# Linear attention in pieces between the units of softmax attention, and a merge added in PSUM

## The chip, the cores and the metric

One core of a Trainium2 chip runs the whole model in one launch. The metric is the device time of the kernel in microseconds; three runs of the kernel before took 2956.83, 2958.68 and 2958.93 us, so their median is 2958.68.

## The reference

Two models run one after the other on 256 tokens of width 1024. The first has 16 meta tokens ahead (272 rows) and two layers, each of feed-forward, mixer, feed-forward; the second has a convolution, sparse attention and two mixtures of 64 experts, and is not touched here. The change is in the first model's mixer and in the norm ahead of it.

```python
def mixer(z, ...):
    h = z @ w_in                       # z = rmsnorm of the residual stream
    (q_a, k_a, v_a, r_a, lr_f, lr_b, q_b, k_b, v_b, g_a, g_b) = jnp.split(h, SPLIT_POINTS, axis=-1)
    a = gla_branch(q_a, k_a, v_a, r_a, lr_f, lr_b, ...)      # linear attention, 4 heads, both directions
    b = attention_branch(q_b, k_b, v_b, ...)                 # softmax attention, 8 heads, 2 key heads
    y = (jax.nn.sigmoid(g_a + b_merge[0]) * (a @ w_pa)
         + jax.nn.sigmoid(g_b + b_merge[1]) * (b @ w_pb))
    return y @ w_out
```

In the linear branch each head (keys of 64, values of 128) is worked out in chunks of 64 tokens: masked scores of queries against keys inside a chunk, and a state S that is decayed and added to from chunk to chunk, once forwards and once backwards. The sum of the two directions is divided by the root of its mean square over the head's 128 values, multiplied by a gain and by silu(r).

## The kernel before, in words

All is float32. Activations lie with features on partitions and the 272 tokens in the free dimension, a tensor of width 1024 as eight tiles of 128 x 272. The five engines have one instruction stream each, written out by hand in one order; semaphores join them. `products` on TensorE runs groups of matmuls into one PSUM bank and then signals it full; `claim` waits until the reader of a bank has freed it. A float32 matmul shows in the trace as two rows.

The feed-forward parts, the merge's projections and the output projection split each number into a rounded high part and a low rest and add three fast products (`split_sum`, its matmuls are line 537). Their weights come in column chunks: SyncE loads a label of the plan into one of three ring buffers once the label three before it is used up, ScalarE rounds a chunk to its high part (`high_part`, line 1073), GpSimd subtracts that from the weights (`low_parts`, line 1826), TensorE multiplies. There are high buffers for three chunks, so chunk c + 3 starts when chunk c is used up. For the feed-forward part the last stage is the down projection: four column pairs c, each in two halves h, two tiles dt. VectorE adds each finished tile to the residual H (line 1450), ScalarE squares it (line 1077).

The mixer of a layer then goes, on TensorE:

- `rms_norm`: `column_means` multiplies the eight squared tiles by a matrix of 1/1024 (line 569) into bank 7; ScalarE takes the root (line 1097), VectorE the reciprocal and the normed tiles (lines 1400 and 1402).
- The projections of w_in, 98 us, and beside them the decays of the linear branch on ScalarE and VectorE. In layer 0 ScalarE also issues eight stores of a bias table (line 1166).
- Softmax attention in 24 units, a head by three tiles of its rows (128, 128, 16). Step n of the loop issues the scores of unit n + 1, the transposes of unit n - 1 (`turn_rows`, line 511), the value products of unit n - 2 (`values`, line 708), and in two of three steps one whole gate tile (`gate_tile`, 8 matmuls of 272 columns). VectorE takes the row maximum (line 1513), ScalarE the exponential (line 1222), VectorE scales it (line 1520) and copies the transposes. The value products of a pair of heads gather in bank 4 or 5. ScalarE turns each gate tile into a sigmoid (line 1171).
- Linear attention, all behind the last unit: transposed decayed keys in three banks, chunk scores of either direction in two (masked on VectorE, line 1535), the meta tokens' scores, the chunk states (chained on VectorE, line 1555), then the outputs of the four heads (line 791) in four banks, 18 small matmuls each, one set over rows 0 to 63 and one over rows 64 to 127.
- The norm of the heads: ScalarE squares each head (line 1237), four products with a matrix of 1/128, four square roots, and per head on VectorE a reciprocal (line 1560), the scaling (line 1562), a rounded and an unrounded product with silu(r) (lines 1564, 1565) and their difference (line 1566).
- The merge: column pair kk of a @ w_pa and of b @ w_pb in turn, four banks. Per tile VectorE multiplies both by their gates (lines 1571 and 1573), adds them (line 1574), rounds the sum (line 1575) and subtracts (line 1576). Then the output projection, eight tiles in banks 4 to 7, added to H (line 1581).

## Time and profile before

| | before |
|---|---|
| runs, us | 2956.83, 2958.68, 2958.93 |
| profiled execution, us | 2959.34 |
| its span, us | 2957.5 |
| mean granted TensorE clock | 0.944 |
| busy, share of the span | TensorE 90%, weight loads 68%, VectorE 35%, ScalarE 31%, GpSimd 31% |
| chain that ended last | TensorE 76%, DMA 11%, VectorE 9%, ScalarE 2% |

The span runs from the first instruction to the last. Matmul and weight load are two rows of one engine and overlap. The granted clock is a share of 2.4 GHz and has two levels, 1.00 and 0.50 (1.2 GHz); a number between them is a mean over a stretch. The chain that ended last is followed backwards from the last instruction, at each step to what released it.

### The profile page before, as it was taken

What the parts mean: (1) busy time and instruction counts of PE and PEld (TensorE: products, weight loads), DVE (VectorE), ACT (ScalarE), POOL (GpSimd) and SP (SyncE); (2) the same over time, 40 slices, a digit from 0 to 9 for tenths busy, and PEclk for the clock granted to TensorE, in tenths of its full rate; (3) what the DMA queues carried; (4) which work ended last, traced back from release to release, by engine and by line L of the source; (5) the groups of instructions that cost most, each with busy time, mean ns of one, the idle gap of its engine ahead of it and who ended that gap; (6) DMA issues with size and microseconds to landing.
All of it is one profiled execution on the core that took longest, in us unless ns stands there. A gap on an engine that the chain in (4) does not pass through costs nothing.

```text
span 2957.5 us, 44948 instructions
## 1 busy us (share of the span) xinstructions
PE 2649.1 (90%) x18090; PEld 2025.6 (68%) x18090; DVE 1049.0 (35%) x2379; ACT 907.9 (31%) x1477; POOL 902.6 (31%) x373
## 2 busy tenths in 40 slices
PE   8999897899999999789989699999878678999996
PEld 8996566899999756679989644444457574444443
DVE  3402424643441152364317333232324623323233
ACT  4431461343443136234433121211113521121112
POOL 6860001588788000147868100000014240000000
PEclk9999996999999999689999799999988988999999
DMA  7553410454554322035545499999952156999995
GB/s 244 160 166 111 128 63 23 132 180 148 182 176 155 127 86 86 29 99 158 164 143 168 171 394 421 421 421 421 421 193 101 43 204 244 421 421 421 421 421 218
DMA packets 271164, 643.95 MB, mean 218 GB/s; under 512 B 16816, under 2 KB 191024, under 8 KB 221616
## 3 DMA queue, kind: packets, MB, share of 16 engines
q1 hardware_dynamic: 267952, 635.66, 57.2%
q10 hardware_dynamic: 2176, 3.15, 0.4%
q0 software_dynamic: 896, 3.15, 0.3%
q8 instruction: 104, 1.70, 0.2%
q14 instruction: 36, 0.29, 0.0%
HBM read 637.72 MB, written 4.19 MB: 217 GB/s over the span
## 4 chain that ended last, share of the span: by engine, by line
PE 76%; DMA 11%; DVE 9%; ACT 2%; issue 1%; SPq 0%; ACTq 0%; POOL 0%; DVEq 0%
PE bank L537 35%; PE bank L501 15%; DMA wring<-in_exp_w 11%; PE bank L997 6%; PE bank L982 5%; PE bank L958 3%; PE bank L1006 3%; PE bank L971 3%; PE bank L791 2%; PE bank L569 2%; PE bank L708 1%; PE bank L511 1%; DVE ARENA L1776 1%; DVE XN_rounded L1425 1%; DVE ARENA_rounded L1576 1%
## 5 line engine op out<-in xcount | busy, mean ns | idle before, releaser
L1826 POOL TENSOR_TENSOR wring_rounded<-wring,wring_rounded 128x1024 fp32r<-128x1024 f32 (+1 forms) x336 | 874.1, 2615 | 438.5 <-ACT wring_rounded L1073 437.8
L537 PE MATMUL bank<-SQ_rounded,wring_rounded 128*128 128x272 f32 (+1 forms) x3456 | 653.7, 289 | 28.4 <-POOL wring_rounded L1826 17.8
L537 PEld LDWEIGHTS bank<-SQ_rounded,wring_rounded 128*128 128x128 f32 x3456 | 545.2, 190 | 30.7 <-POOL wring_rounded L1826 13.8
L1073 ACT ACTIVATE wring_rounded<-wring 128x1024 fp32r<-128x1024 f32 (+1 forms) x336 | 374.5, 1117 | 425.8 <-PE bank L537 420.3
L537 PE MATMUL bank<-XN_rounded,wring_rounded 128*128 128x272 f32 (+1 forms) x1728 | 497.5, 288 | 0.0
L537 PE MATMUL bank<-ARENA_rounded,wring_rounded 128*128 128x272 f32 (+1 forms) x3456 | 446.7, 293 | 56.1 <-DVE ARENA_rounded L1566 27.2
L537 PEld LDWEIGHTS bank<-ARENA_rounded,wring_rounded 128*128 128x128 f32 x3456 | 444.1, 194 | 59.6 <-DVE ARENA_rounded L1566 28.5
L537 PEld LDWEIGHTS bank<-XN_rounded,wring_rounded 128*128 128x128 f32 x1728 | 328.7, 190 | 0.2
L997 PE MATMUL bank<-wring,ARENA 128*32 128x512 f32 x2048 | 248.0, 602 | 41.9 <-DVE ARENA L1776 30.4
L1333 ACT ACTIVATE ARENA<-bank 128x512 f32<-128x512 f32 x128 | 76.5, 597 | 662.0 <-PE bank L997 662.0
L501 PE MATMUL bank<-XN,wring 128*128 128x272 f32 (+2 forms) x1088 | 260.1, 405 | 11.8 <-DVE XN L1402 11.8
L982 PE MATMUL bank<-ARENA 64*128 64x512 f32 x1008 | 250.4, 615 | 0.0
L501 PEld LDWEIGHTS bank<-XN,wring 128*128 128x128 f32 (+2 forms) x1088 | 191.2, 181 | 70.2 <-DVE XN L1402 12.6
L1006 PEld LDWEIGHTS bank<-CST,ARENA 128*128 128x128 f32 x1024 | 130.3, 196 | 109.7 <-ACT ARENA L1333 109.7
L997 PEld LDWEIGHTS bank<-wring,ARENA 128*32 128x32 f32 x2048 | 54.0, 109 | 197.1 <-issue 165.2
L1853 POOL DMA_DIRECT2D ARENA<-bias_table x8 | 6.1, 767 | 553.7 <-DVE H L1414 553.7
L1835 POOL TENSOR_TENSOR ARENA_rounded<-ARENA,ARENA_rounded 128x256 fp32r<-128x256 f32 (+1 forms) x24 | 17.6, 735 | 505.5 <-ACTq L1052 505.5
L958 PEld LDWEIGHTS bank<-ARENA 128*128 128x128 f32 x1024 | 123.9, 198 | 61.5 <-DVE ARENA L1776 34.1
L958 PE MATMUL bank<-ARENA 128*128 128x128 f32 x1024 | 136.3, 288 | 32.0 <-DVE ARENA L1776 27.9
L1006 PE MATMUL bank<-CST,ARENA 128*128 128x32 f32 x1024 | 144.5, 285 | 1.4 <-ACT ARENA L1333 1.4
L1790 DVE TENSOR_TENSOR ARENA<-ARENA,bank 128x64 f32<-128x64 f32 x128 | 28.4, 222 | 329.0 <-ACT ARENA L1338 329.0
L971 PE MATMUL bank<-ARENA 128*32 128x512 f32 x1024 | 133.9, 594 | 4.8 <-issue 4.8
(237 smaller groups left out, 2458.0 us busy)
## 6 DMA issues: line engine op xcount, KB each, us to landing
wring<-in_exp_w SPq DMA_DIRECT2D x256, 1024.0 KB, 18.4
ARENA<-in_exp_w SPq DMA_DIRECT2D x128, 1024.0 KB, 17.0
wring<-in_ffn_w_gate SPq DMA_DIRECT2D x44, 1024.0 KB, 5.5
wring<-in_ffn_w_up SPq DMA_DIRECT2D x44, 1024.0 KB, 8.1
...
```

Of the source, the lines that this page charges most:

```text
L501: ins = nc.tensor.matmul(o, l, r, start=(i == 0), stop=(i == len(g) - 1))
L537: ins = nc.tensor.matmul(o, rounded(a_[:, k, cols]), rounded(x), start=(start and k == 0 and j == 0), stop=(stop and k == len(tiles) - 1 a ...
L569: ins = nc.tensor.matmul(bank[b][:, 0:x.shape[1]], const(wgt), x, start=(k == 0), stop=(k == len(tiles) - 1))
L791: ins = nc.tensor.matmul(o, l_, r_, start=(r0 == 0 and i == 0), stop=(r0 == 64 and i == len(by_row[64]) - 1), skip_group_check=True)
L958: ins = nc.tensor.matmul(GATHER[:, kk * P:(kk + 1) * P], XTOK[:, t, k * P:(k + 1) * P], GS[:, t, :], start=(t == 0), stop=(t == 1))
L971: ins = nc.tensor.matmul(DOWN[32 * q:32 * q + 32, :], HT[:, c * 32:c * 32 + 32], w2[:, c, dh * 512:dh * 512 + 512], start=True, stop=True, ...
L982: ins = nc.tensor.matmul(bank[2 * t + dh][:, :], PUT[64 * dh:64 * dh + 64, u % 2, t * P:(t + 1) * P], YS[64 * dh:64 * dh + 64, :], start=f ...
L997: ins = nc.tensor.matmul(UP[32 * q:32 * q + 32, :], XG[:, k, u * 32:u * 32 + 32], v[:, :, k, :], start=(k < 4), stop=(k >= 4), tile_positi ...
L1006: ins = nc.tensor.matmul(TURN[:, f * 32:f * 32 + 32], half[:, f % 2, :], const("sum4"), start=True, stop=True)
L1073: st.done(A(rounded(high), w_, ACT.Copy), wh_ready)
L1333: A(HS[:, :], UP[:, :], ACT.Copy).then_inc(m.hs, 1)
L1826: st.done(nc.gpsimd.tensor_tensor(rounded(low), low, part(high), ALU.subtract), wl_ready)
```

## The change: what it does

1. The down projection of a feed-forward part takes the means of squares two tiles at a time: after the first half of column pair c the two squared tiles of pair c - 1, and the last two after the end. This holds for all parts but layer 0's second, and so also for the last one, ahead of the second model. ScalarE takes up the square root's table ahead of the last two squares.
2. A gate tile is issued in quarters of two matmuls. Eight quarters go ahead of attention's loop, then two or three per step between scores, transposes and value products, and one in each of the two last steps. Bank 4 alone holds the value products, banks 5 and 6 the gates.
3. The sigmoid becomes (1 + tanh(x / 2)) / 2: ScalarE takes a tanh with scale 0.5 and a halved bias; VectorE adds the 1 where it multiplies by the gate, and the factor 1/2 of both gates goes into the addition to H.
4. Linear attention is cut into pieces that use bank 7: transposed keys behind steps 1 to 3, chunk scores behind 4 and 5, the meta tokens' scores behind 6, the states behind 7 to 10, the head outputs in two parts each from step 11 to 18. VectorE adds the masked scores of both directions, and so a head has 14 matmuls. ScalarE squares each head, VectorE multiplies it by silu(r) at once.
5. The four heads' mean squares are four groups of 32 rows of one bank in step 24, one square root and one reciprocal serve all, and four products of one row of ones with a row of the result spread them over 128 partitions.
6. w_pb is loaded, split and multiplied ahead of w_pa. Its column pairs 0 and 1 run before the spreading products, 2 and 3 behind them, then w_pa's. VectorE multiplies w_pb's results by their gates, works out the heads' high and low parts, and later multiplies w_pa's results by their gates in PSUM and adds w_pb's; ScalarE rounds the sum (line 1575's work). The output projection waits tile by tile for its first chunk.

```diff
+        tall(("pb", l), w["w_pb"][l], 4)
         tall(("pa", l), w["w_pa"][l], 4)
-        tall(("pb", l), w["w_pb"][l], 4)
...
-GATE_STEPS = [n for n in range(24) if n % 3 != 2]
+STEPS = 26
+QUARTERS_FIRST = 8
+QUARTERS = [2 + (n % 4 == 3) if n < 24 else 1 for n in range(STEPS)]
+GATES_DONE = [range((QUARTERS_FIRST + sum(QUARTERS[:n])) // 4, (QUARTERS_FIRST + sum(QUARTERS[:n + 1])) // 4)
+              for n in range(STEPS)]
+KEY_STEPS = (1, 2, 3)
+SCORE_STEPS = (4, 5)
+META_STEP = 6
+STATE_STEPS = (7, 8, 9, 10)
+OUT_STEPS = (12, 14, 16, 18)
+MEAN_STEP = 24
+GATE_BANKS, WOVEN_BANK = (5, 6), 7
...
+                        if c > 0 and h == 0 and (l, j) != (0, 1):
+                            column_means(7, "mean_d", rows(SQ)[2 * c - 2:2 * c], "act", 2 * c - 2)
+                if (l, j) != (0, 1):
+                    column_means(7, "mean_d", rows(SQ)[KD - 2:], "act", KD - 2)
...
+            def gate_quarters(l):
+
+                for g in range(16):
+                    v, b, m = cols_of(("gate", l, g // 4), 512), GATE_BANKS[g % 2], g % 4
+                    claim(b)
+                    for k in range(KD):
+                        ins = nc.tensor.matmul(bank[b][:, 0:T], v[:, k, m * P:(m + 1) * P], XN[:, k, :], start=(k == 0),
+                                               stop=(k == KD - 1))
+                        if k in (1, 3, 5):
+                            yield
+                    st.done(ins, bank_full["act"][b])
+                    held[b] = "act"
+                    if m == 3:
+                        used(("gate", l, g // 4))
+                    yield
...
+                for _ in range(QUARTERS_FIRST):
+                    next(gates)
...
-                    hp, b = 64 * (h % 2), 4 + h // 2 % 2
+                    hp, b = 64 * (h % 2), 4
...
+                        rc, t, at = 64 * (c % 2), c // 2, c * 64
+                        o = WB[:, at:at + 64]
+                        by_row[rc].append((o, VA[rc:rc + 64, t, h * P:h * P + P], ATT[rc:rc + 64, 2 * h + t, :]))
...
+                def head_means():
+                    st.need(sq_ready, 4)
+                    products(0, "act", "act", [[(bank[0][32 * h:32 * h + 32, 0:T], const("mean128")[:, 0:32], OSQ[:, h, :])]
+                                               for h in range(4)])
...
+                for n in range(STEPS):
+                    quarters = QUARTERS[n]
+                    if n + 1 < len(units):
+                        scores(n + 1)
+                    next(gates)
+                    if 1 <= n <= len(units):
+                        turn_rows(n - 1)
+                    if quarters > 1:
+                        next(gates)
+                    if n >= 2:
+                        values(n - 2)
+                    if quarters > 2:
+                        next(gates)
+                    if n == KEY_STEPS[0]:
+                        st.need(gla_ready)
+                    if n in KEY_STEPS:
+                        keys_turned(KEY_STEPS.index(n))
+                    if n in SCORE_STEPS:
+                        chunk_scores(SCORE_STEPS.index(n))
+                    if n == META_STEP:
+                        meta_scores()
+                    if n in STATE_STEPS:
+                        states(STATE_STEPS.index(n))
+                    if n + 1 in OUT_STEPS:
+                        head_out(OUT_STEPS.index(n + 1), 0)
+                    if n in OUT_STEPS:
+                        head_out(OUT_STEPS.index(n), 64)
+                    if n == MEAN_STEP:
+                        head_means()
...
+                for kk in range(2):
+                    gated_products(kk, pairs(BTH, BT, 4), (lambda k: st.need(xl_ready)) if kk == 0 else None)
+                st.need(d2p)
                 for h in range(4):
-                    b = (0, 1, 6, 7)[h]
-                    st.need(sq_ready)
-                    products(b, "act", None, [[(bank[b][:, 0:T], const("mean128"), SQ[:, h, :])]])
-
+                    b = (6, 7, 0, 1)[h]
+                    products(b, "dve", "dve", [[(bank[b][:, 0:T], const("ones")[32 * h:32 * h + 1, :],
+                                                 OSTD[32 * h:32 * h + 1, :])]])
+                for kk in range(2, 4):
+                    gated_products(kk, pairs(BTH, BT, 4))
                 st.need(d2p)
-                st.need(xl_ready, 4)
                 for kk in range(4):
-                    for m, tiles in enumerate((pairs(ATH, AT, 4), pairs(BTH, BT, 4))):
-                        for i in range(2):
-                            b = 2 * i + m
-                            claim(b)
-                            chunk_done(split_sum(bank[b][:, 0:T], tiles, cols=slice(i * P, i * P + P), again=(i == 1)),
-                                       bank_full["dve"][b])
-                            held[b] = "dve"
-                st.need(d2p)
+                    gated_products(kk, pairs(ATH, AT, 4))
+                tiles = pairs(GAH, GA, KD)
                 for k in range(KD):
-                    split_products(4 + k % 4, "dve", pairs(GAH, GA, KD))
+                    b = 4 + k % 4
+                    claim(b)
+                    chunk_done(split_sum(bank[b][:, 0:T], tiles, before=(lambda i: st.need(y_ready)) if k == 0 else None),
+                               bank_full["dve"][b])
+                    held[b] = "dve"
+
+            def gated_products(kk, tiles, before=None):
+                for i in range(2):
+                    b = 2 + 2 * (kk % 2) + i
+                    claim(b)
+                    chunk_done(split_sum(bank[b][:, 0:T], tiles, before=before if i == 0 else None,
+                                         cols=slice(i * P, i * P + P), again=(i == 1)), bank_full["dve"][b])
+                    held[b] = "dve"
...
-                st.done(A((GA, GB)[g // 8][:, g % 8, :], bank[b][:, 0:T], ACT.Sigmoid,
+                st.done(A((GA, GB)[g // 8][:, g % 8, :], bank[b][:, 0:T], ACT.Tanh, scale=0.5,
...
+                    if n - 1 in OUT_STEPS:
+                        h = OUT_STEPS.index(n - 1)
+                        st.need(bank_full["act"][WOVEN_BANK])
+                        st.done(A(OSQ[:, h, :], bank[WOVEN_BANK][:, 0:T], ACT.Square), sq_ready)
+                        squared[l, h] = st.last
+                    if n in (22, 23, 24):
+                        high_part()
+                st.need(bank_full["act"][0])
+                st.done(A(OSTD, bank[0][:, 0:T], ACT.Sqrt, bias=const("eps_rms")), a2d)
+                mark(bank_free["act"][0])
                 for i in range(15):
                     high_part()
+                    if 4 <= i < 8:
+                        for k in (2 * i - 8, 2 * i - 7):
+                            st.need(y_sum)
+                            st.done(A(rounded(GAH[:, k, :]), GA[:, k, :], ACT.Copy), y_high)
...
+                        then(TT((ATT, ATT2)[d], WB[:, :].rearrange("p (a b) -> p a b", a=8),
+                                bcast(const(("low", "high")[d]), 8), ALU.mult), bank_free["dve"][WOVEN_BANK])
+                        if d == 1:
+                            st.done(TT(ATT, ATT, ATT2, ALU.add))
...
+                        dve.wait_ge(*squared[l, h])
+                        st.done(TT(AT[:, h, :], WB[:, 0:T], RA[:, h, :], ALU.mult), bank_free["dve"][WOVEN_BANK])
+
+                st.need(a2d)
+                st.done(v.reciprocal(OSTD, OSTD), d2p)
+
+                def gated(kk):
+                    for i in range(2):
+                        b, k = 2 + 2 * (kk % 2) + i, 2 * kk + i
+                        st.need(bank_full["dve"][b])
+                        st.done(STT(GB[:, k, :], GB[:, k, :], 1.0, bank[b][:, 0:T], ALU.add, ALU.mult),
+                                bank_free["dve"][b])
+
+                def head_scaled(h):
+                    b = (6, 7, 0, 1)[h]
                     g = small("gla_gn")[:, l * 4 + h:l * 4 + h + 1]
-                    then(STT(AT[:, h, :], bank[2 + h][:, 0:T], g, SQ[:, 4 + h, :], ALU.mult, ALU.mult),
-                         bank_free["dve"][2 + h])
-                    then(TT(rounded(ATH[:, h, :]), AT[:, h, :], RA[:, h, :], ALU.mult))
-                    then(TT(AT[:, h, :], AT[:, h, :], RA[:, h, :], ALU.mult))
+                    st.need(bank_full["dve"][b])
+                    st.done(STT(rounded(ATH[:, h, :]), AT[:, h, :], g, bank[b][:, 0:T], ALU.mult, ALU.mult))
+                    then(STT(AT[:, h, :], AT[:, h, :], g, bank[b][:, 0:T], ALU.mult, ALU.mult), bank_free["dve"][b])
                     st.done(TT(rounded(AT[:, h, :]), AT[:, h, :], part(ATH[:, h, :]), ALU.subtract),
                             None if h < 3 else d2p)
-                for k in range(KD):
-                    b = 2 * (k % 2)
-                    st.need(bank_full["dve"][b])
-                    st.done(TT(GA[:, k, :], GA[:, k, :], bank[b][:, 0:T], ALU.mult), bank_free["dve"][b])
-                    st.need(bank_full["dve"][b + 1])
-                    then(TT(GB[:, k, :], GB[:, k, :], bank[b + 1][:, 0:T], ALU.mult), bank_free["dve"][b + 1])
-                    then(TT(GA[:, k, :], GA[:, k, :], GB[:, k, :], ALU.add))
-                    then(v.tensor_copy(rounded(GAH[:, k, :]), GA[:, k, :]))
-                    st.done(TT(rounded(GA[:, k, :]), GA[:, k, :], part(GAH[:, k, :]), ALU.subtract),
-                            None if k < KD - 1 else d2p)
+
+                for kk in range(2):
+                    gated(kk)
+                for h in range(4):
+                    head_scaled(h)
+                for kk in range(2, 4):
+                    gated(kk)
+                for kk in range(4):
+                    two = [(2 + 2 * (kk % 2) + i, 2 * kk + i) for i in range(2)]
+                    for b, k in two:
+                        st.need(bank_full["dve"][b])
+                        st.done(STT(bank[b][:, 0:T], GA[:, k, :], 1.0, bank[b][:, 0:T], ALU.add, ALU.mult))
+                    st.settle()
+                    for b, k in two:
+                        st.done(TT(GA[:, k, :], bank[b][:, 0:T], GB[:, k, :], ALU.add), y_sum)
+                    for b, k in two:
+                        mark(bank_free["dve"][b])
+                    for b, k in two:
+                        st.need(y_high)
+                        st.done(TT(rounded(GA[:, k, :]), GA[:, k, :], part(GAH[:, k, :]), ALU.subtract), y_ready)
...
-                    st.done(TT(H[:, k, :], bank[b][:, 0:T], H[:, k, :], ALU.add), h_tile)
+                    st.done(STT(H[:, k, :], bank[b][:, 0:T], 0.5, H[:, k, :], ALU.mult, ALU.add), h_tile)
```

## Rows read from the trace of the kernel before

**Rows 1.** By stretch: length; PE, PEld, DVE, ACT, POOL busy (instructions); clock; DMA share; GB/s.
```profile
200.00:219.30 19.30, 19.30 (x156) 19.30 (x155) 0.88 (x2) 3.96 (x6) 9.66 (x3) 1.00 0.55 172
...
327.30:341.50 14.20, 5.03 (x22) 3.61 (x21) 4.79 (x10) 6.03 (x12) 0.00 (x0) 0.79 0.92 273
341.50:443.70 102.20, 102.20 (x500) 69.81 (x500) 29.96 (x117) 62.19 (x99) 2.28 (x3) 0.98 0.24 80
443.70:455.40 11.70, 7.77 (x158) 5.81 (x157) 7.82 (x21) 3.64 (x5) 7.75 (x4) 0.98 0.38 143
455.40:503.20 47.80, 33.83 (x153) 31.62 (x153) 14.45 (x20) 4.74 (x9) 0.00 (x0) 0.54 0.00 0
503.20:542.30 39.10, 27.64 (x192) 26.98 (x192) 28.35 (x40) 8.48 (x8) 19.35 (x8) 0.89 0.20 71
542.30:568.70 26.40, 26.38 (x192) 26.39 (x193) 13.84 (x12) 12.39 (x19) 15.94 (x7) 0.91 0.43 135
1084.10:1094.50 10.40, 5.01 (x21) 3.59 (x20) 4.76 (x9) 5.97 (x12) 0.00 (x0) 0.94 0.59 202
1094.50:1197.40 102.90, 102.86 (x500) 70.22 (x500) 30.00 (x117) 62.23 (x99) 2.28 (x3) 0.97 0.19 67
...
1197.40:1258.40 61.00, 43.85 (x311) 38.66 (x309) 22.26 (x41) 8.38 (x14) 7.74 (x4) 0.54 0.07 27
1258.40:1326.40 68.00, 56.54 (x385) 55.89 (x386) 42.38 (x52) 20.86 (x27) 35.02 (x15) 0.86 0.29 93
```

**Rows 2.** TensorE's waits, 441 to 573: us in total, times, longest.
```profile
PE bank L537 <- DVE ARENA_rounded L1566: 13.7, 1, 13.7
PE bank L537 <- DVE ARENA_rounded L1576: 5.9, 1, 5.9
```

**Rows 3.** Instructions in time, TensorE: gate tiles one period apart (start, us).
```profile
352.09 3.94 PE L501 MATMUL bank<-XN,wring 128*128 128x272 f32 x16
...
365.31 3.93 PE L501 MATMUL bank<-XN,wring 128*128 128x272 f32 x16
```

**Rows 4.** Instructions in time, TensorE: keys, scores, states, head outputs.
```profile
443.73 1.53 PE L511 MATMUL bank<-CST,ARENA 128*128 128x128 f32 x12
...
445.19 3.19 PE L501 MATMUL bank<-ARENA 64*64 64x64 f32 x80
...
448.31 3.82 PE L501 MATMUL bank<-ARENA,SQ 16*64 16x128 f32 x64
...
455.40 30.38 PE L791 MATMUL bank<-ARENA 64*128 64x64 f32 x144 [3.28 <-DVE ARENA L1555]
```

**Rows 5.** ScalarE's groups, 341 to 443: count, busy us, mean ns.
```profile
L1171 ACT ACT_TABLE_LOAD x16 | 20.5, 1283 | 0.5
```

**Rows 6.** Instructions in time, VectorE: a head's reciprocal and scaling.
```profile
488.12 1.85 DVE L1560 RECIPROCAL SQ<-SQ 128x272 f32<-128x272 f32 x1 [32.87 <-ACT SQ L1097]
490.01 0.50 DVE L1562 SCALAR_TENSOR_TENSOR ARENA<-bank,SM,SQ 128x272 f32<-128x272 f32 x1
```

**Rows 7.** VectorE's groups by shape, 503 to 543.
```profile
L1576 DVE TENSOR_TENSOR ARENA_rounded<-ARENA,ARENA_rounded 128x272 fp32r<-128x272 f32 x8 | 9.8, 1230 | 0.3
...
L1573 DVE TENSOR_TENSOR ARENA<-ARENA,bank 128x272 f32<-128x272 f32 x8 | 3.5, 431 | 6.8 <-PE bank L537 6.8
```

**Rows 8.** GpSimd's groups, 503 to 543.
```profile
L1826 POOL TENSOR_TENSOR wring_rounded<-wring,wring_rounded 128x1024 fp32r<-128x1024 f32 x8 | 19.4, 2419 | 67.8 <-ACT wring_rounded L1073 67.8
```

**Rows 9.** Instructions in time: the norm ahead of layer 0's mixer, TensorE and ScalarE.
```profile
219.27 3.83 PE L569 MATMUL bank<-SQ,CST 128*128 128x272 f32 x16
219.94 0.43 ACT L1077 ACTIVATE SQ<-H 128x272 f32<-128x272 f32 x1 [3.72 <-DVE H L1450]
...
223.14 0.49 ACT L1097 ACTIVATE RS<-bank,CST 128x272 f32<-128x272 f32 x1 [1.46 <-PE bank L569]
```

**Rows 10.** Instructions in time, ScalarE: layer 0's first exponential.
```profile
340.66 0.49 ACT L1222 ACTIVATE ARENA<-bank,ARENA 128x272 f32<-128x272 f32 x1 [8.07 <-issue]
```

**Rows 11.** The chain of waits in time, in a feed-forward part: start, us, count.
```profile
577.05 198.81 PE bank L537 x1584
```

232 lines of the change are left out of this document (111 added, 121 removed).

## The prediction

> **What bounds the kernel now.** First the chain of waits of the whole span: three quarters of it is TensorE, 11% the transfers of the expert weights, so an edit counts where it takes time from TensorE's own row, or idle time from between its rows. The diff touches only the two layers' mixers and the tails of the feed-forward parts ahead of them, so next comes the busy time by stage [rows 1]. The reader is to see three kinds of stage there. In attention (341.5 to 443.7) TensorE is busy for 102.2 of 102.2 us at clock 0.98: bound by TensorE. In linear attention (455.4 to 503.2) it is busy for 33.8 of 47.8 us, and at clock 0.54, its lower level: nothing else works, and what it does takes twice its time. In the merge (503.2 to 542.3) it is busy for 27.6 of 39.1 us. Then TensorE's waits [rows 2]: 13.7 and 5.9 us are the longest, both for VectorE. Last the order in time [rows 3, 4] for the price of each piece.
>
> From the first scores to the end of the output projection a mixer takes 14.2 + 102.2 + 11.7 + 47.8 + 39.1 + 26.4 = 241.4 us in layer 0 and 10.4 + 102.9 + 61.0 + 68.0 = 242.3 in layer 1 [rows 1].
>
> **Start of attention.** Before: two score products and one gate tile, then a wait for the first exponential. One gate tile is 3.86 us (a period of 13.22 us holds two, and what is not gate is three steps' work) [rows 3]. After: two whole tiles and two quarters go first, so 2.5 tiles stand in the gap, 11.0 us with the scores. In layer 1 the gap of 10.4 becomes 11.1. In layer 0 ScalarE is held by its table stores until 340.7 [rows 10] and now does two gates of 0.49 us before the first exponential, so 14.2 becomes 15.2. In return 1.5 tiles, 5.8 us, leave the loop. The loop's work at full clock is 8 x 13.22 = 105.7, less 1.1 for the scores and 3.9 for the tile already done: 100.8; the rows have 102.2 and 102.9, so 1.4 and 2.1 us are the low clock after the gap. Layer 0: 15.2 + 95.0 + 1.4 = 111.6 against 116.4, a gain of 4.8. Layer 1 has no gap left: 11.1 + 95.0 = 106.1 against 113.3, a gain of 7.2. Does any engine replace TensorE in a step? Its three steps of a period take 4.4 us each, gates included; from scores to scaled row it is 0.4 + 0.5 + 0.2 + 0.4 and handovers, near 3 us, and the order allows it two steps. VectorE has 30 us of work in 102 [rows 1] and gets about 1 us more per woven step.
>
> **Gates in quarters.** The same 16 matmul rows per tile, but 48 more changes from one kind of work to another per mixer. A change that waits costs about 0.2 us (a tile of 16 rows takes 3.86 where 16 x 0.227 = 3.63). The added ones wait for nothing, a case that no row shows: between 0 and 9.6 us. I take 2.5, near the low end, since the weight loads can run ahead.
>
> **Gates as tangents.** Before, ScalarE reloads a table for each gate and again for the exponential after it, 1.28 us each [rows 5], 16 times each. It has 62 us of work in 102, so nothing on TensorE's path waits for it; if all these loads go, nothing is gained, and if they stay, the first exponential comes up to 2.6 us later in each layer. I take 0. The Trainium skill (ScalarE: Activation LUTs, "Table sets: the hidden batching unit") puts tanh into exp's set; by that all loads go. No run here shows it yet, and by it the sum stays as it is; without it the sum would be 5 us more.
>
> **Linear attention between units.** Per piece, from rows at full clock [rows 4]: turned keys 12 rows in 1.5 us; scores 80 rows in 3.2; states 64 rows in 3.8. The head outputs ran at half clock, 144 rows in 30.4, 211 ns each. The change adds the two directions' score matrices on VectorE first, so 18 matmuls per head become 14, 112 rows in all. At full clock a row lies between 105 ns (half of 211) and 128 ns (a transposing row, 1.53 / 12): 12 to 14 us; I take 12. Each of the 18 pieces starts behind one more wait, 18 x 0.2 = 3.6. Means of squares, once for four heads: 8 rows of 272 columns, between 0.5 and 2 us; 1. Together 1.5 + 3.2 + 3.8 + 12 + 3.6 + 1 = 25.1, or 24.6 since the pauses inside the states are counted in both. With the quarters 27.1 us, against 11.7 + 47.8 = 59.5 and 61.0: gains of 32.4 and 33.9. Also gone with it: four square roots, four reciprocals of 1.85 us [rows 6] and the 13.7 us wait.
>
> What the woven pieces queue behind: TensorE's woven group of step n waits for VectorE to have emptied bank 7 of step n - 1, which it does early in step n; no wait. With one bank for the value products, the next pair of heads waits for two copies of 0.4 us, two pieces later: hidden.
>
> **Merge.** Time 0 is TensorE's last value product. A column chunk of a projection is 24 rows of 0.1255 us at full clock [rows 11], 3.01, with its start 3.05. Chunks pb0 and pb1 run at once; the fourth head pair arrives 1.8 us late (two copies, one subtraction on GpSimd), 0.6 us idle: to 6.7. Four broadcasts of the deviation, 2.6: 9.3. pb2, pb3: 15.4. VectorE: square root and reciprocal to 5.2, two gate products each for kk 0 and 1 to 7.2, then four heads of 0.5 + 0.5 + 0.44. The 0.44 is a subtraction with both inputs in SBUF; beside GpSimd's 2.42 us weight subtraction [rows 8] such a one takes 1.23 us on average, while one that reads PSUM stays at 0.43 [rows 7]. Heads end at 16.3, and the bank for pa0 is free at 16.8: 1.4 idle. Chunks pa0 to pa3 end at 19.9, 23.0, 26.0 and, after 0.5 for a bank, 29.6. Here VectorE falls behind: per chunk 2 x 0.5 + 2 x 0.43 + 0.2 from PSUM, then two subtractions of about 1.2: 4.3 us against 3.05. The last of four is done at 19.9 + 4 x 4.3 = 37.1; the output's first chunk can't end before 37.9. Seven more are 21.4, and the low clock after such a wait costs 2.0 (the eight chunks took 26.4 behind the 5.9 us wait, not 24.4). Sum 61.3, against 65.5 and 68.0: gains of 4.2 and 6.7. Bounds: no block of GpSimd's costs anything and no clock is lost, 53; every subtraction waits a full 2.4, 66.
>
> The rule of the Trainium skill that bears on this (SBUF — State Buffer, its part on ports and contention: a VectorE instruction with two SBUF inputs contends with one of GpSimd that reads SBUF, one with at most one SBUF input does not) agrees with 1.23 against 0.43. By it the sum added in PSUM is never held up, and only the subtraction is.
>
> Order pb before pa moves two 2 MB loads; each comes two thirds into attention and lands in 7 to 8 us, long before its chunk. The output weights' first load now starts at time 0 and is wanted after 18 us: hidden.
>
> **Norm means tile by tile.** Three tails: both mixers' and the last norm's. TensorE is busy for 19.3 of 19.3 us ahead of them [rows 1], so the six matmuls moved forward cost their 6 x 0.46 = 2.75 us there. Behind, the eight took 3.8 us and the square root came at 223.1, though the last square was ready at 220.4 [rows 9]. Now it can come at 221.1 to 221.3: 1.9 saved. A loss of about 1 each, 3 in all (between -1 and +2 each). The early table load hides nothing that was bare in the mixers.
>
> **Sum.** Layer 0: 4.8 + 32.4 + 4.2 = 41.4. Layer 1: 7.2 + 33.9 + 6.7 = 47.8. Less 3: 86.2. The profiled execution took 2959.3 us (1.8 around its span), 0.6 over the median of the runs. 2959.3 - 86.2 = 2873.1; I take 2873 for the median too. Costs of unknown size: quarters -5 to +14, heads 0 to +4, merge -17 to +9, norms -6 to +3, table loads 0 to +5.
>
> **Rivals.** (1) The clock does not hold. The small matmuls of linear attention kept TensorE busy for 34 us and its clock stayed at 0.50 to 0.54 [rows 1]; in layer 1 it had fallen already during the states (0.54 over 61 us). For it: that. Against: the steps without a gate keep full clock, and every woven step still has two quarters. The Trainium skill (TensorE: Matmul & The Clock Gate, "What's actually happening") lets a busy engine return to full clock; this trace differs, busy without a return. Price: a woven step at half clock costs its length again, about 6 us. If only the eight head-output steps suffer half of their time: 2 x 20 more, 2914. If all steps from the states on run at half clock, 12 x 4.4 + 17.4 = 70 us twice over: 2873 + 140 = 3013, slower than before. It decides from 43 us of half clock per mixer. (2) GpSimd and VectorE meet less in the merge, since blocked subtractions fall into each other's waits and the quarters' changes are free: 2 x (61.3 - 54) + 5 = 19.6: 2853. (3) The steps are bound by the handovers, not by TensorE, and the weave fills idle time: excluded by busy 102.2 of 102.2. (4) The change doesn't shorten anything because the saved time returns as a wait for weights: the loads take 0.24 of the DMA's time in attention; 2955, hardly.
>
> **How the numbers follow.** Forecast with its own range 2860 to 2890: 0.58. Rival 2: 0.21. Half clock in part: 0.14. In full, slower: 0.04. Rival 4 and the rest: 0.03. The range takes in rival 2 and part of rival 1: 2845 to 2908. 0.2%, 6 us, is what a measurement can tell from no change. Faster 0.95, same 0.01, slower 0.04.
>
> **What would show it.** The gap before the loop at most 4 us in layer 0 and none in layer 1; steps of 4.4 us, woven ones near 6, at clock over 0.95; head rows near 105 ns; no table loads in the loop; last value product to the output's first row near 30 us, with a wait for VectorE's subtractions ahead of the output; tails where the square root follows the last square within 0.8 us. Wrong if the clock of the woven steps is under 0.9, or if TensorE idles inside them.

## The result and the profile after

Four runs of the changed kernel took 2903.77 to 2908.53 us, median 2907.38; four of the kernel before on the same chip 2956.83 to 2959.82, median 2958.8. The ratio is 0.983, with an interval of [0.9815, 0.9843]: 51 us faster, where 86 were forecast. The time lies inside the range of 2845 to 2908, at its slow end, and outside the forecast's own range of 2860 to 2890.

| | before | after |
|---|---|---|
| profiled execution, us | 2959.3 | 2908.5 |
| its span, us | 2957.5 | 2906.3 |
| mean granted TensorE clock | 0.944 | 0.955 |
| busy us: TensorE, VectorE, ScalarE | 2649, 1049, 908 | 2634, 1028, 831 |
| its chain | TensorE 76%, DMA 11%, VectorE 9%, ScalarE 2% | TensorE 77%, DMA 11%, VectorE 8%, ScalarE 2% |

Cut at instructions that both kernels have, the 51.2 us of the two spans come out as follows ("loop and weave" runs from TensorE's first attention scores to its last value product, and before to the end of linear attention; after the change two gate tiles, 7.5 us, stand ahead of the scores):

| stretch | before, us | after, us | gain forecast | gain measured |
|---|---|---|---|---|
| norm ahead of layer 0's mixer | | | -1 | -1.3 |
| layer 0: projections, two gate tiles | 98.3 | 105.5 | | |
| layer 0: loop and weave | 175.9 | 150.7 | 37.2, with the line above | 17.9 |
| layer 0: merge and output | 65.6 | 60.3 | 4.2 | 5.3 |
| up to layer 1's mixer | 416.2 | 417.0 | -1 | -0.8 |
| layer 1: projections, two gate tiles | 99.2 | 105.7 | | |
| layer 1: loop and weave | 174.3 | 130.8 | 41.1, with the line above | 37.0 |
| layer 1: merge and output | 68.0 | 60.2 | 6.7 | 7.8 |
| up to the second model | 216.5 | 217.4 | -1 | -0.9 |
| second model (not touched) | 1414.6 | 1428.4 | 0 | -13.8 |

So layer 1 gained 44.8 of 47.8 us, layer 0 only 23.2 of 41.4, and the second model, in which no line was changed, gave 13.8 back.

The busy time by stretch of the kernel after, columns as in [rows 1]: the start of attention, loop and weave, merge and output of layer 0, then the same of layer 1.

```profile
327.30:346.00 18.70, 13.68 (x51) 10.05 (x50) 5.13 (x10) 6.99 (x15) 0.00 (x0) 0.84 0.86 245
346.00:486.60 140.60, 136.91 (x754) 92.81 (x753) 43.00 (x142) 25.10 (x70) 9.32 (x6) 0.88 0.14 50
486.60:546.80 60.20, 52.64 (x393) 51.50 (x393) 41.15 (x57) 26.69 (x40) 35.82 (x16) 0.94 0.42 140
...
1061.00:1072.70 11.70, 11.70 (x51) 8.93 (x49) 4.79 (x10) 6.88 (x14) 0.00 (x0) 1.00 0.52 179
1072.70:1200.30 127.60, 123.92 (x754) 84.55 (x753) 43.25 (x143) 25.30 (x72) 9.32 (x6) 0.97 0.14 50
1200.30:1260.50 60.20, 52.79 (x395) 51.54 (x394) 41.22 (x57) 26.65 (x40) 35.81 (x16) 0.94 0.42 140
```

Both second rows run from the second scores to the last value product, and the two loops hold the same instructions. They differ in the clock: a mean of 0.88 means that 24% of 140.6 us, 34 us, ran at the lower level and lost half of that, 17; a mean of 0.97 means 6% of 127.6, 3.8 lost. The difference, 13, is what lies between the two lengths. The 47.8 us at 0.54 of [rows 1] are gone in both.

TensorE's waits in layer 0 after, from the start of attention to the end of the value products (engine and line, what it waited for: us, times, longest), to be read against [rows 2]:

```profile
PE bank L645 <- ACT ARENA L1239: 5.0, 1, 5.0
PE bank L810 <- DVE ARENA L1649: 2.2, 1, 2.2
PE bank L515 <- DVE ARENA L1600: 1.1, 1, 1.1
PE bank L551 <- POOL ARENA_rounded L1946: 0.3, 1, 0.3
```

Line 645 is a gate's quarter, 1239 its tanh; 810 a head's output, 1649 VectorE's product of a head with silu(r), which frees bank 7; 515 is attention's scores, 1600 the reciprocal that frees their bank. The prediction had none of the first three.

### The profile page after: what moved, and what is told of

Read it like the earlier page. It is cut to its first block, busy times and chain, and to the rows that moved or that the text cites. A ratio compares the mean times of both kernels' runs of the same rounds, so it can differ in the third digit from the quotient of the medians.

```text
span 2906.3 us, 44807 instructions
## 1 busy us (share of the span) xinstructions
PE 2634.4 (91%) x18042; PEld 1994.5 (69%) x18042; DVE 1028.2 (35%) x2360; ACT 830.6 (29%) x1428; POOL 901.9 (31%) x373
## 4 chain that ended last, share of the span: by engine, by line
PE 77%; DMA 11%; DVE 8%; ACT 2%; issue 1%; SPq 0%; ACTq 0%; POOL 0%; DVEq 0%
PE bank L551 35%; PE bank L515 11%; DMA wring<-in_exp_w 11%; PE bank L1064 6%; PE bank L1049 5%; PE bank L645 5%; PE bank L1025 3%; PE bank L1073 3%; PE bank L1038 3%; PE bank L584 2%; PE bank L737 1%; PE bank L810 1%; DVE ARENA L1887 1%; DVE XN_rounded L1503 1%; PE bank L525 1%
## 5 line engine op out<-in xcount | busy, mean ns | idle before, releaser
L551 PEld LDWEIGHTS bank<-SQ_rounded,wring_rounded 128*128 128x128 f32 x3456 | 546.1, 190 | 30.8 <-POOL wring_rounded L1937 13.8
L1946 POOL TENSOR_TENSOR ARENA_rounded<-ARENA,ARENA_rounded 128x256 fp32r<-128x256 f32 (+1 forms) x24 | 17.6, 735 | 534.6 <-ACTq L1118 534.6
L645 PE MATMUL bank<-XN,wring 128*128 128x272 f32 x512 | 157.3, 439 | 5.0 <-ACT ARENA L1239 5.0
L1038 PE MATMUL bank<-ARENA 128*32 128x512 f32 x1024 | 135.2, 599 | 11.2 <-issue 11.2
L515 PE MATMUL bank<-XN,wring 128*128 128x272 f32 (+2 forms) x576 | 130.5, 402 | 11.8 <-DVE XN L1480 11.8
```

Source lines behind the costliest of these rows:

```text
L515: ins = nc.tensor.matmul(o, l, r, start=(i == 0), stop=(i == len(g) - 1))
L551: ins = nc.tensor.matmul(o, rounded(a_[:, k, cols]), rounded(x), start=(start and k == 0 and j == 0), stop=(stop and k == len(tiles) - 1 a ...
L645: ins = nc.tensor.matmul(bank[b][:, 0:T], v[:, k, m * P:(m + 1) * P], XN[:, k, :], start=(k == 0), stop=(k == KD - 1))
L1038: ins = nc.tensor.matmul(DOWN[32 * q:32 * q + 32, :], HT[:, c * 32:c * 32 + 32], w2[:, c, dh * 512:dh * 512 + 512], start=True, stop=True, ...
```

## Where the time went in the trace

**The start of attention in layer 0.** TensorE and then ScalarE in order of time (start, us, and in brackets the idle time ahead and its releaser):

```profile
328.46 7.50 PE L645 MATMUL bank<-XN,wring 128*128 128x272 f32 x32
335.88 1.18 PE L515 MATMUL bank<-ARENA 64*128 64x272 f32 x4
342.09 3.96 PE L645 MATMUL bank<-XN,wring 128*128 128x272 f32 x8 [5.02 <-ACT ARENA L1239]
345.99 1.05 PE L515 MATMUL bank<-ARENA 64*16 64x272 f32 x2
```

```profile
335.15 6.26 ACTq L1234 DMA_DIRECT2D bias_table<-RW  x2
341.46 0.86 ACT L1239 ACTIVATE ARENA<-bank,SM 128x272 f32<-128x272 f32 x2 [7.58 <-issue]
342.21 0.49 ACT L1292 ACTIVATE ARENA<-bank,ARENA 128x272 f32<-128x272 f32 x1
```

The third gate tile's first quarter needs bank 5, which holds the first tile until its tanh. That tanh stands on ScalarE behind the issue of the bias table's stores. The forecast saw ScalarE late at this place, but hung only the exponential on it; the quarters, which it had filling the gap, wait for it too, and run at half clock behind it: 8 rows in 3.96 us, where layer 1 takes 2.10. The second scores come at 346.0; 328.5 and the forecast 15.2 give 343.7.

**A wait inside a woven step.** All engines, weight loads left out, around step 13 of layer 0 (a head's second part is in it, and the copy of the first head pair):

```profile
413.09 0.62 PE L737 MATMUL bank<-ARENA 128*64 128x16 f32 x6
413.74 0.40 ACT L1298 ACTIVATE ARENA<-bank 128x272 f32<-128x272 f32 x1 [7.98 <-PE bank L737]
414.04 0.39 ACT L1299 ACTIVATE ARENA_rounded<-bank 128x272 fp32r<-128x272 f32 x1
...
414.56 0.49 ACT L1239 ACTIVATE ARENA<-bank,SM 128x272 f32<-128x272 f32 x1
414.94 0.39 ACT L1307 ACTIVATE ARENA<-bank 128x272 f32<-128x272 f32 x1
415.36 0.44 DVE L1649 TENSOR_TENSOR ARENA<-bank,ARENA 128x272 f32<-128x272 f32 x1 [8.20 <-ACT ARENA L1307]
...
415.86 1.20 PE L810 MATMUL bank<-ARENA 64*128 64x64 f32 x8 [2.15 <-DVE ARENA L1649]
```

ScalarE's stream has the copies of a finished head pair (1298, 1299) ahead of the square of the head (1307). The copies need the value products of the step that is still running (737). So ScalarE stood idle for 8 us, though the head was whole in bank 7 from 410.2 on, squared it last, VectorE freed the bank last, and TensorE, which wants that bank for the next head, idled for 2.15 us. At the second head pair the same order makes VectorE, which waits for the square, late with a reciprocal: the 1.1 us.

**The clock in layer 0's loop.** Stretches of 10 us after, columns as in [rows 1]:

```profile
412.00:422.00 10.00, 7.85 (x37) 5.51 (x35) 3.19 (x11) 3.09 (x9) 0.76 (x1) 0.83 0.00 0
422.00:432.00 10.00, 10.00 (x45) 6.69 (x44) 1.48 (x6) 0.98 (x3) 0.00 (x0) 0.67 0.00 0
432.00:442.00 10.00, 10.00 (x34) 7.63 (x34) 0.86 (x3) 1.06 (x3) 0.00 (x0) 0.50 0.01 2
442.00:452.00 10.00, 10.00 (x43) 6.96 (x41) 2.42 (x8) 1.46 (x4) 0.00 (x0) 0.64 0.04 7
452.00:462.00 10.00, 10.00 (x53) 7.23 (x53) 1.13 (x5) 0.58 (x2) 0.00 (x0) 0.88 0.53 203
```

The clock falls in the head-output steps and is at its lower level from 425.4 to 449.3, so for all of the row from 432 to 442. It is back while head outputs still run. This long stretch begins 10 us behind the wait of 2.15 us and ends ahead of the one of 1.1 us, which stands at 466.3; so of the two only the first can have brought it. TensorE is busy for 10.00 of 10.00 us in four of the five, the wait at 415.9 being in the other. The Trainium skill (TensorE: Matmul & The Clock Gate, "What's actually happening") has a busy engine return to full clock; this stretch, like the one of [rows 1], doesn't bear that out.

The product rows of the same woven group, the first part of the third head, after, in layer 0 and then in layer 1:

```profile
433.82 5.59 PE L810 MATMUL bank<-ARENA 64*128 64x64 f32 x24
...
1154.71 3.08 PE L810 MATMUL bank<-ARENA 64*128 64x64 f32 x24
```

At full clock a row is 128 ns, the upper of the two bounds (105 to 128); 112 rows are 14.3 us where 12 were taken.

**The merge.** VectorE after, in order of time: the difference of a head (1667) beside GpSimd's subtractions, the gate product on PSUM (1680), the sum (1683), the subtraction of the sum (1688).

```profile
495.08 2.31 DVE L1667 TENSOR_TENSOR ARENA_rounded<-ARENA,ARENA_rounded 128x272 fp32r<-128x272 f32 x1
...
498.24 0.44 DVE L1667 TENSOR_TENSOR ARENA_rounded<-ARENA,ARENA_rounded 128x272 fp32r<-128x272 f32 x1
...
510.95 0.79 DVE L1683 TENSOR_TENSOR ARENA<-bank,ARENA 128x272 f32<-128x272 f32 x2
512.00 2.70 DVE L1688 TENSOR_TENSOR ARENA_rounded<-ARENA,ARENA_rounded 128x272 fp32r<-128x272 f32 x2 [0.26 <-ACT ARENA_rounded L1319]
```

The split of [rows 7] holds: those that read a bank are never held (0.39 to 0.50 each), those with both inputs in SBUF take 0.44 when free and 1.7 to 2.3 us beside GpSimd.

**The second model.** TensorE after: the first product behind the exit of either of the two loops over experts, and the last norm. Before, in the same view, the first two had waits of 2.41 and 2.35 us, and the last norm took 3.72 us.

```profile
2100.63 1.94 PE L1038 MATMUL bank<-ARENA 128*32 128x512 f32 x8 [5.82 <-issue]
...
2869.91 1.93 PE L1038 MATMUL bank<-ARENA 128*32 128x512 f32 x8 [5.43 <-issue]
...
2887.03 6.76 PE L584 MATMUL bank<-SQ,CST 128*128 128x256 f32 x16 [2.83 <-ACT SQ L1171]
```

"issue" is a wait for nothing that the profile shows. The two exits cost 6.5 us more than before, and the last norm, now at half clock, 3.0. That clock is not the exits' doing alone: in before_pad26 below the second exit takes 5.66 us and the last norm 3.72 as before.

## The experiments

Theory A: the 35 us are missing because TensorE waits inside the woven steps, for bank 7 behind ScalarE's order, and in layer 0 for the first tanh behind the stores; the waits are 8 us, and the clock that falls with them the rest. Theory B: the woven steps are too thin in dense work to hold the clock, wait or no wait. For the second model: the place of TensorE's instructions in its program changed.

**again.** The changed kernel itself, nothing edited.

> The changed kernel once more, unaltered, for a second trace. Both theories of the shortfall say what part of it is fixed. Theory P (placement in time): the stretch at the lower TensorE clock that the head outputs of layer 0 suffered (402 to 463, some 15 us lost) and layer 1 mostly did not (about 4 us) falls differently from run to run, since the same instructions lie in both layers; expected here: layer 0 from first gate tile to last value product between 140 and 158 us against 158.1, layer 1 between 134 and 150 against 138.0. Theory F (fixed): both are within 1 us of 158.1 and 138.0. The two waits at the exit of the expert loops (5.8 and 5.4 us against 2.4 and 2.35 before) stay as they are if the code's placement sets them, and change if they are chance. Time 2904 to 2909.

2907.84 us (2899.02 to 2908.92), ratio 0.981 [0.978, 0.984]; span 2906.7. Loop and weave of layer 0: 157.1 us (150.7 in the first trace); of layer 1: 130.75 in both. The clock of layer 0 varies from trace to trace, layer 1 is steady; every other stretch agrees within 0.4 us but the second model (1423.2 against 1428.4).

**sq_first.** On ScalarE the square of a head goes ahead of the head pair's copies.

```diff
+                    if n - 1 in OUT_STEPS:
+                        ...            # wait for bank 7, square, signal
                     if 2 <= n < STEPS and units[n - 2][1] == 2 and units[n - 2][0] % 2 == 1:
                         ...            # the copies of a head pair
                     if n > 0:
                         ...            # gate tiles
-                    if n - 1 in OUT_STEPS:
-                        ...
```

> ScalarE squares a finished head before it copies the pair of softmax heads, which waits for value products of the step that is still running. The waits of 2.15 and 1.07 us in each layer are to go (6.4 us in all). Theory A: those waits also let the clock fall, so the low stretches behind them go as well, layer 0's loop falls from 158 to about 142, layer 1's from 138 to 131, and the time to 2907 - 6 - 15 = about 2886. Rival B: the sparse head-output matmuls make the clock fall by themselves; then only the 6 us are gained, 2901, and clock under 0.9 remains in head-output steps.

2893.41 us (2892.1 to 2902.79), ratio 0.978 [0.975, 0.981]. Both waits are gone: the first part of the next head starts at 413.25, behind the value products and with no idle time, and of TensorE's waits in layer 0 the first tanh's 4.9 is left with the 0.3. Loop and weave: 136.1 and 128.9 us. So 3.2 us of waits brought 14.6 us in layer 0 (21 against the repeat) and 1.9 in layer 1, where the clock did not rise (0.96, and 0.97 with the waits). Nearly the same stretches as above:

```profile
410.00:420.00 10.00, 10.00 (x61) 7.49 (x60) 3.27 (x11) 2.49 (x8) 0.76 (x1) 1.00 0.00 0
420.00:430.00 10.00, 10.00 (x53) 7.14 (x52) 1.48 (x6) 1.84 (x5) 0.00 (x0) 0.83 0.00 0
430.00:440.00 10.00, 10.00 (x50) 6.93 (x49) 3.20 (x11) 2.04 (x6) 0.00 (x0) 0.83 0.07 8
440.00:450.00 10.00, 10.00 (x60) 7.21 (x60) 2.95 (x11) 0.97 (x3) 0.00 (x0) 1.00 0.50 204
```

The woven work is the same and the clock is 0.83 to 1.00. Theory A holds for the long stretch; what B says is left as short dips. The other runs bear it out. Five kernels have the waits, so ten loops: in four of them, all of layer 0 (the changed kernel, its repeat, stores_early, norm_whole), the clock lies at its lower level for 20 to 24 us on end. Six kernels have the square first, so twelve loops, and none has such a stretch; the longest is 13.7 us. So here the long stretch comes only with the waits, and not every time with them.

**stores_early.** The bias table's eight stores are issued one by one among ScalarE's squares and copies ahead of attention.

```diff
-                if l == 0:
-                    store_bias_rows()
 ...
                     st.done(A(S2[:, i, :], bank[4 + i][:, 0:T], ACT.Square), a2d)
+                    if l == 0:
+                        store_bias_rows(i)
                 for m in range(4):
                     copy(QK[:, m, :], m, bank[m][:, 0:T])
+                    if l == 0:
+                        store_bias_rows(4 + m)
```

> The changed kernel with only the stores moved into the projections, the square still behind the pair's copy. It asks why layer 0's loop suffered 144 to 157 us in four runs where layer 1's took 130.8 three times. Theory: the 5 us wait for the first tanh in layer 0 with its low clock starts it off; without it both loops go alike, layer 0 130 to 132 us. Rival: the waits of 2.2 and 1.1 us bring the long low stretches in layer 0 whatever stood ahead: 140 to 150 us, only 7 less than before.

2900.78 us (2899.93 to 2901.63), ratio 0.980 [0.978, 0.982]. The 5.0 us wait is gone, the 2.2 and 1.1 are not. Loop and weave of layer 0: 143.3, so 7.4 less, near the wait (5.0) and the half clock of the quarters behind it (3.96 less 2.10); the repeat had 157.1, so the size is good to some us only. The clock over the loop is still 0.88, with one low stretch of 24 us in it. So the gap at the start is not what brings the long low stretch. The square first on top of this (next run) takes it away.

**sq_stores.** Both edits.

> Square first, and ScalarE issues layer 0's eight bias-table stores one by one during the projections instead of ahead of the first exponential. My reckoning: TensorE's wait of 4.9 us for the first gate's tanh in layer 0 goes, with the low clock behind it (2 us), so first scores to merge in layer 0 falls from 136.1 to about 129, as in layer 1; the projections stay at 105.4. Rival: the stores hold up ScalarE's copies in the projections, TensorE waits there for banks and the projections take 5 us more or beyond.

2882.27 us (2880.97 to 2883.58), ratio 0.973 [0.970, 0.975]. Loop and weave: 128.9 and 128.9 us, so layer 0 is like layer 1 at last, and 14.4 us shorter than in stores_early, of which 3.2 are waits. From the first gate tile to the second scores layer 0 takes 10.6 us, as layer 1 does. TensorE's waits from 325 to 470, then the start of attention and the two loops:

```profile
PE bank L551 <- POOL ARENA_rounded L1948: 0.3, 1, 0.3
```

```profile
327.30:336.00 8.70, 8.70 (x38) 6.72 (x37) 3.26 (x6) 6.05 (x11) 0.00 (x0) 1.00 0.71 241
...
334.70:463.60 128.90, 128.43 (x765) 87.30 (x764) 46.34 (x150) 26.52 (x75) 9.31 (x6) 0.96 0.14 50
...
1047.20:1176.00 128.80, 128.33 (x765) 87.13 (x764) 46.43 (x150) 26.52 (x75) 9.33 (x6) 0.96 0.14 50
```

**dense_q.** With the square first, three quarters in each of the steps 11 to 18, taken from steps 3, 7, 19, 21, 23.

```diff
-QUARTERS = [2 + (n % 4 == 3) if n < 24 else 1 for n in range(STEPS)]
+QUARTERS = [2, 2, 2, 2, 2, 2, 2, 2, 2, 2, 2, 3, 3, 3, 3, 3, 3, 3, 3, 1, 2, 1, 2, 2, 1, 1]
```

> Square ahead of the pair's copy, as in the run before, and the gate quarters laid out anew: three in each of the eight head-output steps (11 to 18), two in the others, one in 19, 21, 24 and 25; the amount is the same. Theory B (sparse head-output matmuls let the clock fall, gates beside them hold it): the three low stretches of 3.4 us left in layer 0's steps and two in layer 1's become one or none, loop of layer 0 134 us, of layer 1 127, time 2 to 5 us less. Rival (the falls come where they like): as many low stretches as without.

2896.17 us (2895.48 to 2896.86), ratio 0.977 [0.975, 0.980]. Loop and weave: 139.9 and 132.4 us against 136.1 and 128.9 without it. More dense work beside the head outputs doesn't help: the clock of layer 1's loop is 0.94 with no wait in it, against 0.96. The 3.5 us more in layer 1 are not the quarters' price as such, for combo below has the same quarters and 129.2 there. Theory B fails in this form; whether the later steps, which have fewer quarters now, lose what the others gain is not shown.

**sigmoid.** The gates are sigmoids again, the rest of the change stays; VectorE's instructions keep their form, with 0 added where 1 was and a factor of 1 for 0.5, and the one that halves the bias goes.

```diff
-                st.done(A((GA, GB)[g // 8][:, g % 8, :], bank[b][:, 0:T], ACT.Tanh, scale=0.5,
+                st.done(A((GA, GB)[g // 8][:, g % 8, :], bank[b][:, 0:T], ACT.Sigmoid,
```

> Undoes the tangents: ScalarE takes the sigmoid again (scale 1, full bias; VectorE adds 0 where it added 1, the addition to H has factor 1), all else as changed. My reckoning: 16 to 31 table loads of 1.28 us come back per mixer, hidden beside TensorE in the loop, but 1.3 to 2.6 us more before the first exponential of each layer: time +3 to +5. Rival: in the woven steps ScalarE's order (copy, gate, square) makes the loads visible: waits of TensorE inside the loop grow by over 5 us per layer, time +10 and more.

2907.38 us (2907.07 to 2907.68), ratio 0.982 [0.978, 0.985]: the time of the changed kernel. The loads are back, in layer 1's loop:

```profile
L1239 ACT ACT_TABLE_LOAD x13 | 16.7, 1283 | 0.3
L1292 ACT ACT_TABLE_LOAD x12 | 15.4, 1283 | 0.2
```

Layer 1, the steady one, takes 135.2 us instead of 130.75; the wait for bank 7 there is 3.4 instead of 2.1 and the clock 0.95 instead of 0.97. Layer 0 happened to keep its clock better (144.4 us, 0.92) and hides it. The tangents are worth 4.4 us in layer 1's loop, where the prediction had up to 2.6 a layer as the price without them; in layer 0 the wait for the first gate grew from 5.0 to 6.3.

**norm_whole.** The means of squares are taken in one, as before the change.

```diff
-                        if c > 0 and h == 0 and (l, j) != (0, 1):
-                            column_means(7, "mean_d", rows(SQ)[2 * c - 2:2 * c], "act", 2 * c - 2)
                 if (l, j) != (0, 1):
-                    column_means(7, "mean_d", rows(SQ)[KD - 2:], "act", KD - 2)
+                    rms_norm()
 ...
-                if next_gain is None:
-                    warm(ACT.Sqrt)
```

> Undoes the norm means tile by tile (all eight squares are averaged behind the down projection, no early table load). My reckoning: the three tails get shorter by about 1 us each, so the first norm's end comes 1.0 to 1.4 us earlier, the time falls by 3 us. Rival: the parts moved ahead are hidden and the time grows by 2 us per tail.

2898.85 us (2895.03 to 2902.67), ratio 0.979 [0.975, 0.983]. ScalarE's last square and its root ahead of layer 0's mixer, after and with the means in one:

```profile
223.24 0.43 ACT L1143 ACTIVATE SQ<-H 128x272 f32<-128x272 f32 x1 [3.72 <-DVE H L1528]
224.49 0.49 ACT L1163 ACTIVATE RS<-bank,CST 128x272 f32<-128x272 f32 x1 [0.82 <-PE bank L584]
```

```profile
220.19 0.43 ACT L1141 ACTIVATE SQ<-H 128x272 f32<-128x272 f32 x1 [3.72 <-DVE H L1524]
...
223.38 0.49 ACT L1161 ACTIVATE RS<-bank,CST 128x272 f32<-128x272 f32 x1 [1.46 <-PE bank L584]
```

From the last square to the root it is 1.25 us in pieces and 3.19 in one: the pieces save the 1.9 us that were forecast. But the last square itself comes 3.05 us later (2.75 forecast), as the means moved ahead take their own time there. The mixer's first product comes at 230.34 with the pieces, at 229.24 without, and came at 228.99 before. The stretches up to layer 1's mixer and up to the second model are 0.8 and 0.9 us shorter: 2.8 in all, with 3 forecast. Layer 0's loop took 147.7 us here with nothing changed in it (150.7 and 157.1 above), so the 8.5 us between the medians are not the norms' alone.

**combo.** Square first, stores early, means in one and the quarters of dense_q.

> All four together: square first, quarters laid out anew, stores early, norm means whole. By my reckoning the gains add: 2893.4 - 3 (quarters) - 7 (stores) - 3 (norms) = 2880, clock in both loops over 0.97. Rival: the clock falls at other places instead; 2888 or more.

2884.28 us (2882.6 to 2888.81), ratio 0.974 [0.972, 0.976]: no better than sq_stores. The norms' gain (216.5 us up to the second model, not 217.4, and the like ahead of the mixers) is lost to a second model of 1427.1 (1424.2), to the loops (129.3 and 129.2, not 128.9) and to 0.7 us more in the projections.

**before_pad.** The kernel before with 24 empty instructions at the head of TensorE's stream. They did not come into the program, which has as many TensorE instructions as before (11516), so it is one more run of the kernel before.

> The kernel before with 24 empty instructions at the head of TensorE's stream, where it waits for its first weights anyway: no work is changed, only the place of all later TensorE instructions in memory. Theory: the wait at the exit of each expert loop (2.4 us before, 5.2 to 5.8 in every changed kernel, nothing to wait for but its own instructions) depends on that place; it moves away from 2.4, and the stretch from convolution to end from 1414.6 toward 1423 to 1430. Rival: the exit follows from what the loop's other engines do; it stays at 2.4 and the stretch at 1414.6, time 2958.

2959.03 us (2950.75 to 2968.23), ratio 0.9997 [0.998, 1.001]. The exits: 2.4 and 2.4. Its second model took 1408.1 us where the first trace has 1414.6: of this size is what one trace differs from the next there.

**before_pad26** and **sq_stores_pad.** 26 empty instructions that raise a semaphore, which do stay in the program, in the kernel before (11542 instead of 11516) and in sq_stores (11516 instead of 11490, so that the second model's instructions stand where they did before the change).

```diff
+            for _ in range(26):
+                pe.nop().then_inc(padded, 1)
```

> The kernel before with 26 such instructions, which shift it the other way. Place in memory: its exits leave 2.4 (to something between 1 and 7 us), stretch from convolution to end not 1408 to 1415. Rival: 2.4 and 2.4. If the exits stay at 2.4 here but fall back in the run beside it, the place matters by more than this shift.

> Square first and stores early as in the run before, and 26 empty instructions with a signal at the head of TensorE's stream, while it waits for its first weights. The changed kernels have 26 TensorE instructions fewer than the kernel before (11490 against 11516), so every instruction of the second model lies again where it lay before. Theory (place in memory): the two exits of the expert loops, 5.6 and 5.2 us in all changed kernels, are back at 2.4 each, and the stretch from convolution to end falls from 1424 by 6 to 10 us: time about 2875. Rival (something the loops' other engines do): exits stay over 5, time 2882.

The kernel before with them: 2965.68 us (2959.42 to 2968.2), ratio 1.0018 [1.0008, 1.0028], slower by some 5 us. One of its exits went from 2.4 to 5.7, and its second model took 1420.9 us (1414.6 and 1408.1 without):

```profile
2160.42 1.80 PE L974 MATMUL bank<-ARENA 128*32 128x512 f32 x8 [2.42 <-issue]
...
2929.71 1.94 PE L974 MATMUL bank<-ARENA 128*32 128x512 f32 x8 [5.66 <-issue]
```

sq_stores with them: 2878.44 us (2874.1 to 2882.78), ratio 0.973 [0.970, 0.975], against 0.9726 without, so the times don't tell them apart; in the traces its exits sum to 7.5 us (10.8 without) and its second model took 1417.9 (1424.2). So 26 instructions at the head of TensorE's stream decide over at least one of the two exits, the second; that they do so by the place of what follows is the likeliest reading and not shown by itself. It doesn't explain the first exit, which stayed at 5.4 with TensorE's count restored. The change also altered the streams of ScalarE (1477 profiled instructions before, 1428 after) and VectorE (2379, 2360), and no run pads these.

**best.** Square first, stores early, means in one, the quarters as in the change, 26 padded.

> Square first, stores early, norm means whole, 26 empty instructions. If all parts hold: 2882.3 - 7 (exits) - 2 (norms) = 2873. Rival: the exits stay, 2880.

2871.96 us (2869.79 to 2874.37), ratio 0.970 [0.969, 0.972]; the changed kernel's ratio has the interval [0.9815, 0.9843] and its repeat's [0.978, 0.984], so it is faster than the kernel before and the changed one. Its start of attention, its loops (layer 0, layer 1) and its second exit:

```profile
327.30:335.70 8.40, 8.40 (x38) 6.67 (x37) 2.00 (x4) 5.56 (x10) 0.00 (x0) 1.00 0.73 250
335.70:464.80 129.10, 128.63 (x767) 87.37 (x767) 46.39 (x149) 26.66 (x76) 9.31 (x6) 0.96 0.14 50
...
1048.40:1175.70 127.30, 126.83 (x765) 86.51 (x764) 46.35 (x150) 26.51 (x75) 9.32 (x6) 0.97 0.14 50
```

```profile
2839.49 1.07 PE L1039 MATMUL bank<-ARENA 128*32 128x512 f32 x8 [2.16 <-issue]
```

## Why the prediction was right and wrong, step by step

- **Start of attention.** Layer 1 as forecast: from the first gate tile (1062.1) to the second scores (1072.7) 10.6 us, forecast 11.1, no gap. Layer 0: 17.5 against 15.2. What failed is that 2.5 tiles stand in the gap: the half tile needs the bank that the late tanh frees. With early stores the same span is 10.6 us with no gap.
- **Gates in quarters.** 2.5 us taken, from a range of 0 to 9.6. A change that waits for nothing costs about 0.03 us, 1.5 in all, worked out from three loop steps with six quarters, 11.5 us. Near the low end, as taken.
- **Gates as tangents.** No table load stands in the loop after. Costed at 0, and their lack at up to 2.6 us a layer; the sigmoid kernel shows 4.4 in the steady layer. The Trainium skill's rule on the table sets (ScalarE: Activation LUTs, "Table sets: the hidden batching unit") is borne out: tanh and exp side by side have no load, the sigmoid has 13 and 12. Of the 4.4 the wait at bank 7 has 1.3; the rest is about what the clock lost, 5% of 135.2 us, 6.8, against 3% of 130.7, 3.9.
- **The weave's own work.** From the first gate tile to the last value product layer 1 took 138.2 us, where 11.1 + 95.0 + 27.1 = 133.2 were forecast. Of the 5.0 over, 3.2 are waits. The rest is low clock, 3.9 lost by the mean of 0.97, less what the pieces cost under their forecast. With the waits gone it is 1.6 to 3.2 over: 127.3 from the first scores in best and 128.9 in sq_stores, and 133.2 less the 7.5 of the two tiles ahead of them is 125.7.
- **What the woven pieces queue behind: the step that failed.** It said of bank 7 that VectorE empties it, "which it does early in step n; no wait". It followed VectorE's and TensorE's order and not ScalarE's, whose copies of a head pair need the products of the running step and stand ahead of the square that VectorE waits for. Of these copies it said that they are "hidden"; from the value products they are (no wait of line 737 shows), from bank 7 they are not. The waits are 2.2 and 1.1 us in layer 0 and 2.1 and 1.1 in layer 1; in layer 0 they brought 11.6 to 21 us with the clock (136.1 with the square first, against 147.7, 150.7 and 157.1), in layer 1 1.9. sq_first shows it, and sq_stores against stores_early once more (14.4).
- **The clock, rival 1 in part (0.14).** It named the head-output steps and 20 us a mixer; it came in layer 0 alone, 13 us more than in layer 1. Its 2914 (2913 by its own terms, 2873 and twice 20) lies close to the measured 2907 by luck: it counted 20 us in each mixer, where one lost 13 more than the other, and knew nothing of the second model's 13.8. Its reasoning, that small matmuls as such let the clock fall, is at most a part: the same matmuls without the waits run at 0.96 in both layers. The sign for it in the prediction, a clock under 0.9 or idle time inside woven steps, is what the trace shows in layer 0.
- **Merge.** 61.3 forecast, 60.3 and 60.2 measured; by the trace the parts differ. The heads ended 17.6 us after the last value product, not 16.3, and TensorE idled 4.3 us for it (1.4 forecast); the output projection started at 36.0, behind a wait of 2.9, where the forecast had 34.9 as the earliest; the mean products of the heads cost 0.7 (1.0 forecast) and the broadcasts 0.7 (2.6). Two errors of 2 to 3 us cancel.
- **Norm means.** 3 us lost, 2.8 to 3.1 measured, and right in both terms: 1.9 saved behind the last square, 3.05 lost ahead of it (2.75 forecast).
- **The untouched part.** The sum took it as unchanged. It cost 13.8 us: 6.5 at the exits of the expert loops, 3.0 in the last norm at half clock; the other 4.3 are no more than what one trace of the kernel before differs from another (6.5). A term that nothing in the prediction named, and a quarter of the gain.

Of the 35 us that are missing (86.2 less 50.8 of the profiled executions), 19.3 lie in layer 0's start and loop (37.2 less 17.9) and 13.8 in the second model. In the first the step that failed is the one that put the waits at nothing, and the clock multiplied them; the second was no term at all.

Three things stay open: why layer 0 lost its clock, from 10 us behind a wait of 2.2 us, when layer 1 has the same wait and kept it; why the first exit stayed at 5.4 us with TensorE's instruction count restored; and what about the 26 instructions decides over the second. The order of the pieces' steps (head outputs spread over more steps) was not tried.
